# One 1 MB transfer per chunk of the two expert tables, in place of two of 512 KB

## The chip, the cores and the metric

The kernel runs on one core of a Trainium2 chip. The metric is the device time of one execution in microseconds (us). Before the change the median of three runs is 2290.37 us (2289.84 to 2294.24).

## What is computed

The reference is one layer of a hybrid encoder block on 256 tokens of width 2048, all in float32. The part that the change touches is the last and largest one, the PEER layer:

```python
q = jnp.einsum('bsd,de->bse', x, wq).reshape(B, S, PEER_HEADS, 2, PEER_HALF)
...
vals, pos = lax.top_k(cand, PEER_TOPK)
ids = jnp.take_along_axis(cidx, pos, axis=-1)
gates = jax.nn.softmax(vals, axis=-1)
...
ug = jnp.take(u_tab, ib, axis=0)
vg = jnp.take(v_tab, ib, axis=0)
h = jnp.einsum('td,tkd->tk', xb, ug)
a = (jax.nn.gelu(h.astype(jnp.float32), approximate=False) * gb).astype(xb.dtype)
return jnp.einsum('tk,tkd->td', a, vg)
```

There are 128 x 128 = 16384 experts, each a row of 2048 numbers in the table u and one in the table v, 128 MB a table. Each token picks 128 of them (8 heads, 16 each). The kernel gathers nothing. It computes every token's product with every expert of u, multiplies by a gate that is zero for experts that were not picked, and multiplies the result with all of v. So both tables are streamed once through the matrix engine. The layer before it (input projection, pooling, attention, gates, output projection) streams its weights in the same way.

## The kernel before

**Units and chunks.** Every weight matrix is cut into units of 128 x 1024 floats (512 KB). There are 770 of them, and they pass through one pipeline in one order. Two units are a chunk: 128 experts of u or of v. The tables are 128 chunks each, so 256 units each. Table u has the units from 258, table v (called vtab, in the arrays peer_v) those from 514.

**The pipeline of a unit n.** Float32 products are made of float32r parts, so each unit is split in two.

- SyncE (SP) loads it into RAW slot n % 4 (`load`, L320 to L324). It waits first for `lo_ready`, which says that DVE has finished with the unit that was in this slot, n - 4.
- ScalarE (ACT) copies it to HI slot n % 4 (`conv`, L492 to L498), after its landing and after the matmuls of unit n - 4. I write HI(n).
- VectorE (DVE) subtracts and gives the rest, LO slot n % 2 (`conv`, L832 to L839), after HI(n) and after the matmuls of unit n - 2. I write LO(n). It raises `lo_ready`.
- TensorE (PE) multiplies HI (L1493, in vtab L1511) and then LO (L1499, in vtab L1518), and raises `unit_done`.

**What else stands between these steps.** Each engine takes its instructions in program order. ACT converts three units ahead of PE (`ACT_LEAD`), DVE one ahead (`DVE_LEAD`). In between they take the sums of finished chunks out of PSUM. Chunk c of a phase has the units 2c and 2c + 1, counted from the start of its phase:

- Stage A (first 64 chunks of u). ACT: HI(2c + 4), then the copy of chunk c's sums from PSUM (L740), then HI(2c + 5), then gelu (L748). DVE: LO(2c + 1), a piece of the top-k work, LO(2c + 2), another piece, then the join of chunk c (L947, it adds the second half of the sums and waits for ACT's copy), then LO(2c + 3).
- Stage B (last 64 chunks of u). ACT: HI(2c + 4), then the copy of chunk c's sums to HID (L783), then gelu (L786) after DVE's join. DVE: LO(2c + 2), the join of chunk c (L947), `spread` (L1351), one-hots (L1327 and L1331), the product with the gelu (L1344), then LO(2c + 3). PE also makes gate products (L1788).
- vtab. ACT: `a_hi` (L796), HI, HI. DVE: LO, `a_lo` (L1411), LO. The sums stay in PSUM until the end, so no chunk's sums are taken out.

GpSimd loads small things and clears memory; it is not on the path of the units.

Of the kernel before, what the change touches and what calls it, by code (L numbers as in the profile page):

```python
# [31 lines left out]
NK = 128  # L32
# [10 lines left out]
BASE = {}  # L43
# [64 lines left out]
def hybrid_block_kernel(nc, a, out):  # L108
    with ExitStack() as ctx:
        def sem(name):  # L110
            return ctx.enter_context(nc.semaphore(name))
# [8 lines left out]
        def nxt(name, shape, dt=F32):  # L120
            w = word[0]
            word[0] += -(-int(np.prod(shape[1:])) * mybir.dt.size(dt) // 32) * 8
            return at(name, shape, w, dt)
# [3 lines left out]
        RAW = nxt("raw", [P, 4, UNIT])  # L127
# [91 lines left out]
        raw_in = [sem(f"raw_in{s}") for s in range(4)]  # L219
        hi_ready = sem("hi_ready")  # L220
        lo_ready = sem("lo_ready")
# [77 lines left out]
        def val(i, per, k):  # L299
            return k if i is None else i * per + k  # L300
# [9 lines left out]
        @block.sync  # L310
        def _(sp):
            for tt in range(NT):
                sp.dma_start(X0[:, tt, :], a["x"][tt * P:(tt + 1) * P, :]).then_inc(x_in[tt], 16)
            def norm_cols(q):
                for n in range(2):
                    sp.dma_start(LNG[:, n, q * 512:(q + 1) * 512],
                                 bass.AP(tensor=a["ln_in"].tensor, offset=n * D + q * 512, ap=[[0, P], [1, 512]])
                                 ).then_inc(ln_cols_in[q], 16)

            def load(i, per, u, src):  # L320

                if u >= 4 or i is not None:
                    sp.wait_ge(lo_ready, val(i, per, u - 3))
                sp.dma_start(RAW[:, u % 4, :], src).then_inc(raw_in[u % 4], 16)  # L324

            def load_v(u):
                g, ch = u // 2, u % 2
                if u >= 4:
                    sp.wait_ge(lo_ready, u - 3)
                sp.dma_start(RAW[:, u % 4, :].rearrange("p (b c) -> p b c", b=4),  # L330
                             a["w_in"][24 + 4 * ch:28 + 4 * ch, :, g * 256:(g + 1) * 256]
                             .rearrange("b p c -> p b c")).then_inc(raw_in[u % 4], 16)

            norm_cols(0)
            load_v(0)
            load_v(1)
            norm_cols(1)
            load_v(2)
            load_v(3)
            norm_cols(2)  # L340
            norm_cols(3)
            for u in range(4, 16):
                load_v(u)

            blocks = {"qk": 8, "pool": 0, "gate": 32}

            def src(name, i, c, half):
                cols = slice(half * UNIT, (half + 1) * UNIT)
                k = val(i, 2, c)
                if name in blocks:  # L350
                    return a["w_in"][blocks[name] + k, :, cols]
                if name == "vtab":
                    return a["peer_v"][:, k, cols]
                return a[name][k, :, cols]

            for name, n in PHASES[1:]:
                b = BASE[name]
                if name == "grp":
                    continue
                if name == "gate":  # L360
                    with sp.Fori(0, 14) as i:
                        for j in range(4):
                            load(i, 4, b + j, src(name, i, j // 2, j % 2))
                    for t, (c, half) in enumerate(LAST_GATES):
                        load(None, 4, b + 56 + t, src("grp", None, 0, half) if c is None else src(name, None, c, half))
                    continue
                first = 0
                if name == "branch":
                    for j in range(4):
                        load(None, 4, b + j, src(name, None, j % 2, j // 2))  # L370
                    first = 1
                if name in ("wout", "pleg"):
                    for half in range(2):
                        with sp.Fori(0, KD // 4) as i:
                            for j in range(4):
                                k = i * 4 + j
                                load(i, 4, b + KD * half + j, a[name][k, :, half * UNIT:(half + 1) * UNIT])
                    continue
                with sp.Fori(first, n // 2) as i:
                    for j in range(4):  # L380
                        load(i, 4, b + j, src(name, i, j // 2, j % 2))
            sp.wait_ge(spill_out, 32)
            for tt in range(NT):
                for half in range(2):
                    cols = slice(half * (D // 2), (half + 1) * (D // 2))
                    sp.wait_ge(out_ready, 2 * tt + half + 1)
                    sp.dma_start(out[0, tt * P:(tt + 1) * P, cols], RES2[:, tt, cols]).then_inc(out_done, 16)
            sp.wait_ge(out_done, 16 * 2 * NT)
# [102 lines left out]
        def _(act):  # L491
            def conv(i, per, u):  # L492

                act.wait_ge(raw_in[u % 4], 16 * val(i, per // 4, u // 4 + 1))
                if u >= 4 or i is not None:

                    act.wait_ge(unit_done, val(i, per, u - 3))
                nc.scalar.activation(HI[:, u % 4, :], RAW[:, u % 4, :], ACT.Copy).then_inc(hi_ready, 1)  # L498

            def run(name, iters, per, slots, pre=None, start=0, stop=None):  # L500

                b = BASE[name]

                def body(i):
                    for j in range(per):
                        if pre and j % 2 == 0:
                            pre(i, j // 2)
                        conv(i, per, b + j + ACT_LEAD)
                        if j in slots:
                            slots[j](i)  # L510

                if iters == 1:
                    body(None)
                    return
                with act.Fori(start, iters if stop is None else stop) as i:
                    body(i)
# [12 lines left out]
            nc.scalar.activation(BR[0:HEADS, :], PS[0:HEADS, 0, :], ACT.Copy).then_inc(rel_sb, 1)  # L529
            std_of(1)  # L530
            conv(None, 4, 0)
            xt_hi(0, (0,))
            for u in range(1, 4):
                conv(None, 4, u)
# [1348 lines left out]
```

## Time and profile before

| | |
|---|---|
| median of 3 runs | 2290.37 us |
| profiled execution, its own time | 2288.23 us |
| its span (first to last instruction) | 2286.6 us |
| PE busy | 2241.0 us (98%) |
| DVE busy | 1530.6 us (67%) |
| ACT busy | 1067.3 us (47%) |
| DMA | 425.40 MB, mean 186 GB/s |
| chain that ended last | PE 92%, DVE 4%, issue 2%, DMA 1% |

Busy time is the time in which an engine had an instruction running. The chain that ended last follows the work back from the last instruction, at each step to what released it. PEclk in a row is the TensorE clock that was granted, as a share of full speed. Line numbers are those of the kernel before. L498, L838 and L947 are lines of helpers that serve many places, so a row is told apart by what it writes and reads.

### The profile page before, as it was taken

To read this page: it belongs to the slowest core of one execution; us is meant where nothing else is said; L and a number is where in the kernel's file an instruction comes from. 1 tells how busy PE (TensorE), PEld (TensorE's weight loads), DVE (VectorE), ACT (ScalarE), POOL (GpSimd) and SP (SyncE) were. 2 spreads that over 40 slices of the span, in tenths; PEclk is the share of its full clock that TensorE was granted. 3 is DMA by queue.
4 is the path that set the end of the run, shared out by engine and by line. 5 is a ranking of instruction groups with operands and counts; after the bars stand their busy time and mean duration, and the time that the engine had idled before them with its cause. 6 is when DMAs were issued, how large, how long until landed. Compare 5 with 4: busy or idle time off the path is not lost.

```text
span 2286.6 us, 39059 instructions
## 1 busy us (share of the span) xinstructions
PE 2241.0 (98%) x12096; PEld 1932.4 (85%) x12096; DVE 1530.6 (67%) x2818; ACT 1067.3 (47%) x1483; POOL 45.9 (2%) x93
## 2 busy tenths in 40 slices
PE   7999999999999999999999999999999999999996
PEld 5888888998888888888888888888888888888885
DVE  6457666765744599998888888887555555555556
ACT  3444555654444444445554444444444444444442
POOL 1000000000000000011000000000000000000000
PEclk9999999999999999999999999999999999999998
DMA  7555555557465556565555555555666666666663
GB/s 265 187 189 173 178 183 173 185 196 249 146 192 178 174 185 199 186 210 187 189 160 164 162 163 158 160 163 175 193 192 197 202 205 205 202 202 202 202 192 120
DMA packets 122729, 425.40 MB, mean 186 GB/s; under 512 B 13448, under 2 KB 21656, under 8 KB 121792
## 3 DMA queue, kind: packets, MB, share of 16 engines
q1 hardware_dynamic: 119040, 410.04, 56.1%
q0 software_dynamic: 3648, 14.82, 2.0%
q8 instruction: 25, 0.41, 0.1%
q14 instruction: 16, 0.13, 0.0%
HBM read 420.60 MB, written 6.31 MB: 187 GB/s over the span
## 4 chain that ended last, share of the span: by engine, by line
PE 92%; DVE 4%; issue 2%; DMA 1%; ACT 0%; DVEq 0%; SPq 0%; ACTq 0%
PE ps L1493 29%; PE ps L1511 25%; PE ps L1499 15%; PE ps L1518 13%; PE ps L1788 3%; PE ps L1557 1%; PE ps L1476 1%; PE ps L1481 1%; PE ps L1477 1%; DVE w_lo L838 1%; PE ps L1563 1%; DMA raw<-in_w_in 1%; DVE bn L850 0%; DMA x<-in_x 0%; PE ps L1538 0%
## 5 line engine op out<-in xcount | busy, mean ns | idle before, releaser
L838 DVE TENSOR_TENSOR w_lo<-raw,w_hi 128x1024 fp32r<-128x1024 f32 x770 | 940.3, 1222 | 455.7 <-PE ps L1518 388.9
L498 ACT ACTIVATE w_hi<-raw 128x1024 fp32r<-128x1024 f32 x770 | 815.7, 1061 | 907.0 <-DMA raw<-in_peer_v 372.4
L1493 PE MATMUL ps<-x_t_hi_lo,w_hi 128*128 128x512 f32 x3200 | 815.9, 397 | 1.2 <-DVE experts L947 1.2
L1493 PEld LDWEIGHTS ps<-x_t_hi_lo,w_hi 128*128 128x128 f32 x3200 | 574.0, 189 | 107.1 <-issue 2.7
L1511 PE MATMUL ps<-w_hi,x_t_hi_lo 128*128 128x512 f32 x2560 | 633.2, 389 | 1.3 <-DVE x_t_hi_lo L1411 1.2
L1511 PEld LDWEIGHTS ps<-w_hi,x_t_hi_lo 128*128 128x128 f32 x2560 | 479.8, 188 | 101.0 <-issue 1.8
L1499 PEld LDWEIGHTS ps<-x_t_hi_lo,w_lo 128*128 128x128 f32 x3200 | 435.1, 190 | 38.7 <-DVE w_lo L838 6.8
L1499 PE MATMUL ps<-x_t_hi_lo,w_lo 128*128 128x256 f32 x3200 | 446.8, 282 | 2.3 <-DVE w_lo L838 2.1
L1518 PE MATMUL ps<-w_lo,x_t_hi_lo 128*128 128x512 f32 x1280 | 342.3, 389 | 1.0 <-DVE w_lo L838 1.0
L1518 PEld LDWEIGHTS ps<-w_lo,x_t_hi_lo 128*128 128x128 f32 x1280 | 240.2, 188 | 51.3 <-DVE w_lo L838 1.4
L1788 PE MATMUL ps<-onehots 128*128 128x128 f32 x512 | 77.0, 274 | 0.0
L1331 DVE TENSOR_SCALAR onehots<-iota,i_t,gate_t 128x128 f32<-128x128 bf16 x256 | 76.7, 344 | 0.0
L1788 PEld LDWEIGHTS ps<-onehots 128*128 128x128 f32 x512 | 68.0, 192 | 0.0
L1327 DVE TENSOR_TENSOR onehots<-i_t,iota 128x256 f32<-128x256 bf16 x128 | 53.9, 421 | 19.0 <-DVE experts L1351 14.9
L1411 DVE TENSOR_TENSOR x_t_hi_lo<-experts,x_t_hi_lo 128x256 fp32r<-128x256 f32 x128 | 53.5, 418 | 1.0 <-ACT x_t_hi_lo L796 0.9
L796 ACT ACTIVATE x_t_hi_lo<-experts 128x256 fp32r (+1 forms) x128 | 51.1, 400 | 1.0 <-PE ps L1499 1.0
L947 DVE TENSOR_TENSOR hidden<-ps,hidden 128x256 f32<-128x256 f32 x64 | 27.1, 424 | 28.9 <-ACT hidden L783 28.9
L786 ACT ACTIVATE hidden<-hidden 128x256 f32<-128x256 f32 x64 | 26.8, 419 | 36.5 <-DVE hidden L947 36.5
L783 ACT ACTIVATE hidden<-ps 128x256 f32<-128x256 f32 x64 | 24.6, 384 | 41.0 <-PE ps L1499 40.9
L1351 DVE TENSOR_TENSOR experts<-ps,experts 128x512 f32 (+1 forms) x64 | 43.5, 680 | 0.0
L947 DVE TENSOR_TENSOR gates_t<-ps,gates_t 128x256 f32 (+1 forms) x32 | 13.5, 422 | 41.4 <-ACT gates_t L552 39.8
L947 DVE TENSOR_TENSOR experts<-ps,experts 128x256 f32 x64 | 27.2, 424 | 16.6 <-ACT experts L740 10.6
(214 smaller groups left out, 1126.8 us busy)
## 6 DMA issues: line engine op xcount, KB each, us to landing
raw<-in_u SPq DMA_DIRECT2D x256, 512.0 KB, 4.3
raw<-in_peer_v SPq DMA_DIRECT2D x256, 512.0 KB, 4.7
raw<-in_w_in SPq DMA_DIRECT2D x128, 512.0 KB, 4.3
raw<-in_branch SPq DMA_DIRECT2D x32, 512.0 KB, 4.8
raw<-in_wout SPq DMA_DIRECT2D x32, 512.0 KB, 4.8
raw<-in_pleg SPq DMA_DIRECT2D x32, 512.0 KB, 4.2
raw<-in_wq SPq DMA_DIRECT2D x32, 512.0 KB, 4.2
x<-in_x SPq DMA_DIRECT2D x2, 1024.0 KB, 6.6
```

Source lines behind the costliest of these rows:

```text
L498: nc.scalar.activation(HI[:, u % 4, :], RAW[:, u % 4, :], ACT.Copy).then_inc(hi_ready, 1)
L796: nc.scalar.activation(XH[:, c % 4, :], BUF[:, bass.ds(val(i, 4, c), 1), :].rearrange("p a t -> p (a t)"), ACT.Copy).then_inc(ah_ready, 1)
L838: v.tensor_tensor(LO[:, u % 2, :], RAW[:, u % 4, :], HI[:, u % 4, :].bitcast(F32), ALU.subtract) \
L947: v.tensor_tensor(dst, PS[:, bank, S:2 * S], dst, ALU.add).then_inc(joined, 1)
L1327: ch.tag(v.tensor_tensor(OH[:, n % 2, :, 0, :], both.unsqueeze(2).to_broadcast([P, 2, P]), IOTA[:, :].unsqueeze(1).to_broadcast([P, 2, P]) ...
L1331: ins = v.tensor_scalar(OH[:, n % 2, r, 1, :], IOTA[:, :], I2T[:, bass.ds(t, 1)], GATET[:, bass.ds(t, 1)], ALU.is_equal, ALU.mult)
L1411: v.tensor_tensor(XL[:, c % 4, :], BUF[:, bass.ds(val(i, 4, c), 1), :].rearrange("p a t -> p (a t)"), XH[:, c % 4, :].bitcast(F32), ALU.su ...
L1493: mm(PS[:, bank, :], w(HI, u % 4)[:, k, :], XHL[:, 8 * half + k, :, :].rearrange("p a t -> p (a t)"), start=(half == 0 and k == 0), stop=F ...
L1499: r = mm(PS[:, bank, 0:S], w(LO, u % 2)[:, k, :], XH[:, 8 * half + k, :], start=False, stop=(half == 1 and k == 7))
L1511: mm(nbank(tt, 2 * half + q), stn[:, tt * P:(tt + 1) * P], wh[:, q * 512:(q + 1) * 512], start=(first and s == 0), stop=False, skip_group_ ...
L1518: r = mm(nbank(tt, 2 * half + q), ah[:, tt * P:(tt + 1) * P], wl[:, q * 512:(q + 1) * 512], start=False, stop=last, skip_group_check=True)
L1788: r = mm(PS[:, 4 + g % 2, o:o + P], OH[:, n % 2, t, 0, :], OH[:, n % 2, t, 1, :], start=True, stop=True)
```

## The change

For u and vtab, SP issues one transfer of 128 x 2048 floats (1 MB) per chunk, into the RAW slots of both its units, and ACT waits for the semaphore of the first slot for both. The wait ahead of the transfer is for both slots: `lo_ready` must say that LO of unit u - 3 is done, the unit that was in the second slot. The first chunk of u is still loaded in two parts. All other phases are as before.

```diff
+            def load_chunk(name, i, b, c):
+
+                u = b + 2 * c
+                sp.wait_ge(lo_ready, val(i, 4, u - 2))
+                whole = a["u"][val(i, 2, c)] if name == "u" else a["peer_v"][:, val(i, 2, c), :]
+                sp.dma_start(RAW[:, u % 4:u % 4 + 2, :], whole.rearrange("p (h c) -> p h c", h=2)
+                             ).then_inc(raw_in[u % 4], 16)
+
...
+                if name in ("u", "vtab"):
+                    if name == "u":
+                        load(None, 4, b, src(name, None, 0, 0))
+                        load(None, 4, b + 1, src(name, None, 0, 1))
+                        load_chunk(name, None, b, 1)
+                    with sp.Fori(1 if name == "u" else 0, NK // 2) as i:
+                        load_chunk(name, i, b, 0)
+                        load_chunk(name, i, b, 1)
+                    continue
...
-                act.wait_ge(raw_in[u % 4], 16 * val(i, per // 4, u // 4 + 1))
+                slot = 2 * (u % 4 // 2) if u >= BASE["u"] else u % 4
+                act.wait_ge(raw_in[slot], 16 * val(i, per // 4, u // 4 + 1))
```

SP's instructions in the loop over u before, two chunks an iteration (ISA is the wait for `lo_ready`):

```order
L324 ISA [waits lo_ready]
L324 DMA raw<-in_u 128x1024
L323 REGISTER_ALU
L324 ISA [waits lo_ready]
L324 DMA raw<-in_u 128x1024
L323 REGISTER_ALU
L324 ISA [waits lo_ready]
L324 DMA raw<-in_u 128x1024
L323 REGISTER_ALU
L324 ISA [waits lo_ready]
L324 DMA raw<-in_u 128x1024
```

and in the changed kernel, also two chunks:

```order
L361 ISA [waits lo_ready]
L361 DMA raw<-in_u 128x2048
L359 REGISTER_ALU
L361 ISA [waits lo_ready]
L361 DMA raw<-in_u 128x2048
```

Two of four waits are gone, those that let the first half of a chunk go ahead of the second.

ACT at the start of stage A before. The rows are HI of an even unit (2c + 4), the copy of chunk c's sums, HI of the odd unit (2c + 5), gelu, and the same again:

```order
L498 ACTIVATE w_hi<-raw 128x1024 [waits unit_done,raw_in2]
L740 ACTIVATE experts<-ps 128x256 [waits unit_done]
L498 ACTIVATE w_hi<-raw 128x1024 [waits unit_done,raw_in3]
L748 ACTIVATE experts<-experts 128x256 [waits joined]
L498 ACTIVATE w_hi<-raw 128x1024 [waits unit_done,raw_in0]
L740 ACTIVATE experts<-ps 128x256 [waits unit_done]
```

and the same place in the changed kernel, where L516 is the old L498 and L758 the old L740:

```order
L516 ACTIVATE w_hi<-raw 128x1024 [waits unit_done,raw_in2]
L758 ACTIVATE experts<-ps 128x256 [waits unit_done]
L516 ACTIVATE w_hi<-raw 128x1024 [waits unit_done,raw_in2]
L766 ACTIVATE experts<-experts 128x256 [waits joined]
L516 ACTIVATE w_hi<-raw 128x1024 [waits unit_done,raw_in0]
L758 ACTIVATE experts<-ps 128x256 [waits unit_done]
```

No instruction of ACT has moved; the odd unit now waits for the semaphore of the even one's slot.

DVE in the stage A loop of the changed kernel, from the join of one chunk (L965, before L947) to LO of its odd unit (L856, before L838). DVE's order is the same in both kernels:

```order
L965 ISA [waits act_evac]
L965 TENSOR_TENSOR experts<-ps,experts 128x256
L852 REGISTER_ALU
L856 TENSOR_TENSOR w_lo<-raw,w_hi 128x1024 [waits unit_done,hi_ready]
L1231 MAX tk_v<-tk_s 128x8 x2
```

The join waits for ACT's copy, and the next LO stands right behind the join.

## Rows read from the trace of the kernel before

**Rows 1.** The page: span, and shares of the chain that ended last.

```profile
span 2286.6 us, 39059 instructions
...
PE 92%; DVE 4%; issue 2%; DMA 1%; ACT 0%; DVEq 0%; SPq 0%; ACTq 0%
```

**Rows 2.** Windows: us; busy of PE, PEld, DVE, ACT, POOL; PEclk, DMA share, GB/s.

```profile
1120.00:1530.00 410.00, 408.85 (x2504) 364.72 (x2503) 347.19 (x728) 189.21 (x260) 2.59 (x5) 1.00 0.51 163
1530.00:2230.00 700.00, 698.80 (x3154) 581.13 (x3153) 375.29 (x442) 311.68 (x391) 8.60 (x16) 1.00 0.64 197
```

**Rows 3.** Timeline, stage A: start, us, engine, line, [idle before <-releaser].

```profile
1000.44 1.21 DVE L838 TENSOR_TENSOR w_lo<-raw,w_hi 128x1024 fp32r<-128x1024 f32 x1
1000.95 2.00 PE L1493 MATMUL ps<-x_t_hi_lo,w_hi 128*128 128x512 f32 x8
...
1001.82 11.07 SPq L324 DMA_DIRECT2D raw<-in_u  x5
...
1002.92 1.06 ACT L498 ACTIVATE w_hi<-raw 128x1024 fp32r<-128x1024 f32 x1 [1.41 <-DMA raw<-in_u]
...
1004.05 0.39 ACT L740 ACTIVATE experts<-ps 128x256 f32 x1
...
1005.29 0.43 DVE L947 TENSOR_TENSOR experts<-ps,experts 128x256 f32 x1
...
1005.63 1.22 DVE L838 TENSOR_TENSOR w_lo<-raw,w_hi 128x1024 fp32r<-128x1024 f32 x1
...
1006.54 2.00 PE L1493 MATMUL ps<-x_t_hi_lo,w_hi 128*128 128x512 f32 x8
```

**Rows 4.** Timeline, stage B.

```profile
1506.21 0.38 ACT L783 ACTIVATE hidden<-ps 128x256 f32<-128x256 f32 x1 [0.38 <-PE ps L1499]
...
1506.30 2.09 PE L1493 MATMUL ps<-x_t_hi_lo,w_hi 128*128 128x512 f32 x8
1506.63 0.42 DVE L947 TENSOR_TENSOR hidden<-ps,hidden 128x256 f32<-128x256 f32 x1 [0.26 <-ACT hidden L783]
...
1509.26 1.23 DVE L838 TENSOR_TENSOR w_lo<-raw,w_hi 128x1024 fp32r<-128x1024 f32 x1 [0.19 <-DVE experts L1344]
...
1512.79 2.09 PE L1493 MATMUL ps<-x_t_hi_lo,w_hi 128*128 128x512 f32 x8
1513.12 0.42 DVE L947 TENSOR_TENSOR hidden<-ps,hidden 128x256 f32<-128x256 f32 x1 [0.66 <-ACT hidden L783]
...
1516.15 1.23 DVE L838 TENSOR_TENSOR w_lo<-raw,w_hi 128x1024 fp32r<-128x1024 f32 x1 [0.21 <-DVE experts L1344]
```

**Rows 5.** Landing of the two 1 MB transfers of x at the start.

```profile
DMA to landing us min/median/max: 5.0/6.6/8.2
```

**Rows 6.** Landing of 123 transfers of u in stage B, 512 KB each.

```profile
DMA to landing us min/median/max: 3.4/3.9/5.2
```

**Rows 7.** DMA issues of the page: KB each, median us to landing.

```profile
raw<-in_u SPq DMA_DIRECT2D x256, 512.0 KB, 4.3
raw<-in_peer_v SPq DMA_DIRECT2D x256, 512.0 KB, 4.7
```

**Rows 8.** Timeline, vtab.

```profile
2000.54 1.98 PE L1511 MATMUL ps<-w_hi,x_t_hi_lo 128*128 128x512 f32 x8
2000.81 1.22 DVE L838 TENSOR_TENSOR w_lo<-raw,w_hi 128x1024 fp32r<-128x1024 f32 x1 [1.16 <-PE ps L1518]
...
2002.42 0.40 ACT L796 ACTIVATE x_t_hi_lo<-experts 128x256 fp32r x1
...
2003.26 1.98 PE L1511 MATMUL ps<-w_hi,x_t_hi_lo 128*128 128x512 f32 x8
...
2004.60 0.42 DVE L1411 TENSOR_TENSOR x_t_hi_lo<-experts,x_t_hi_lo 128x256 fp32r<-128x256 f32 x1
```

**Rows 9.** Windows at the end, after the last matmul; columns as in rows 2.

```profile
2265.00:2269.00 4.00, 0.00 (x0) 0.00 (x0) 3.96 (x8) 0.00 (x0) 0.00 (x0) 1.00 0.00 0
2269.00:2286.00 17.00, 0.00 (x0) 0.00 (x0) 14.03 (x19) 0.20 (x1) 0.00 (x0) 0.50 0.31 123
```

## The prediction

> **What bounds the kernel now.** I read the page first. The reader sees there that PE holds 92% of the chain that ended last, of a span of 2286.6 us [rows 1]. The windows by stage say the same of the parts that change: PE is busy 408.85 of 410 us in stage B of u and 698.80 of 700 in vtab, at a clock of 1.00 [rows 2]. So no stall is there to be removed. A change of the loads can gain next to nothing, and the question is whether PE stays fed. For that I read the timeline of a few units in each stage, for the order in which SP, ACT and DVE release each other [rows 3, 4, 8], and then the landing times [rows 5 to 7].
>
> PE spends 1006.54 - 1000.95 = 5.59 us on a chunk in stage A [rows 3], 1512.79 - 1506.30 = 6.49 in stage B [rows 4], and 2 x (2003.26 - 2000.54) = 5.44 in vtab [rows 8].
>
> **What the change removes.** Half of SP's transfers of the tables, 256. SP has nothing else to do in these stages and is not on the chain [rows 1]. Gain: nothing. The bytes are the same.
>
> **What it moves.** The transfer of chunk c + 2 (units 2c + 4 and 2c + 5) now leaves after LO(2c + 1). Before, its first half left after LO(2c), a unit earlier, and was half as long. Three things on the way decide what that costs.
>
> 1. ACT takes HI(2c + 4) right ahead of the copy of chunk c's sums: 1002.92 and 1004.05 in stage A [rows 3]. It takes instructions in order, so the copy waits for the landing.
> 2. DVE's join of chunk c waits for that copy.
> 3. DVE's LO(2c + 3) is behind the join: 1005.29 and 1005.63 [rows 3].
>
> LO(2c + 3) is what the next transfer waits for. So a loop closes over one chunk: LO(2c + 1), transfer, HI, copy, join, LO(2c + 3), next transfer. Before, the same path ran from LO(2c) to LO(2c + 3), three units of PE's time for it, and with the shorter transfer. Now it has two.
>
> **The length X of a 1 MB transfer.** No row shows one of a table. Three nearest rows: the first transfer of x has this size and shape and took 5.0 us from issue to landing, with little beside it [rows 5]. The second, 8.2, lay behind the first. 512 KB of u take 3.4 to 5.2 us in stage B, median 3.9 [rows 6]. To add the second half: the DMA engines move 163 GB/s at a busy share of 0.51 [rows 2], so 320 at full, and 0.52 MB take 1.64 us. That gives 3.4 + 1.64 = 5.0 at best and 3.9 + 1.64 = 5.5 at the median; the median holds transfers that met another one, and in the loop there is only one in flight. I take 5.2, and 4.8 to 5.7 as bounds.
>
> The Trainium skill (DMA: Bandwidth & Descriptors, Measured) has 6.15 us for 1 MB, and a fit of 2.0 us + bytes / 436e3, which is 4.4 us; its rule is to batch transfers to 1 MiB or more. With 6.15 the sum below would be an estimated 120 us longer, with 4.4 an estimated 100 shorter. The row of x lies between them.
>
> **Stage A, one loop.** LO's end to the issue: 1001.82 - 1001.65 = 0.17. X = 5.2. ACT's start after the landing: 0.10 (an allowance; DVE's start behind ACT's copy in rows 4 is of this kind). HI 1.06. Copy 0.07 behind it, 0.39. DVE starts 0.04 later (1506.59 to 1506.63 in [rows 4]). From the join's start to LO's end 1005.29 to 1006.85: 1.56 [rows 3]. Sum 0.17 + 5.2 + 0.10 + 1.06 + 0.07 + 0.39 + 0.04 + 1.56 = 8.6 us, against 5.59 of PE's work. Each chunk costs 3.0 us more. DVE's other work between the joins (the top-k pieces and LO(2c + 2)) is ahead of the join, and fits into the wait for the transfer: from LO's end at 1001.65 to the join at 1005.29 it takes at most 3.6 us [rows 3], and the copy now comes 5.2 + 1.8 = 7.0 us after LO. So that work adds nothing.
>
> **Stage B, one loop.** The same up to the copy (0.38, L783). Behind it DVE has more ahead of LO(2c + 3): join, spread, one-hots, the product. From the join's start to LO's end 1506.63 to 1510.49 = 3.86 and 1513.12 to 1517.38 = 4.26, mean 4.06 [rows 4]. Sum 0.17 + 5.2 + 0.10 + 1.06 + 0.07 + 0.38 + 0.04 + 4.06 = 11.1 us, against 6.49. Each chunk costs 4.6 us more.
>
> **vtab.** No sums are taken out there, so nothing of ACT or DVE for chunk c stands behind a landing of chunk c + 2. Two chunks have 4 slots, so the loop is over two chunks, 10.88 us: issue 0.17, X, 0.10, HI 1.06, a_hi 0.40, a_lo 0.42, two LO at 1.22 [rows 8], together X + 4.6. It is hidden if X is under 6.3. The halves take 4.7 there [rows 7], at 2.72 us from each other, so always two in flight; 4.7 + 1.64 = 6.3 is the upper bound, 5.2 the value as above. I cost vtab at nothing. PE's work hides it, and every 0.1 us over 6.3 would cost 64 x 0.1 = 6 us.
>
> **Sum.** The loop applies from the first full 1 MB transfer on: 65 loops of kind A (one of them with wq's last copy), 64 of kind B. 65 x 3.0 + 64 x 4.6 = 195 + 294 = 489. At the edges of stage B DVE has less between join and LO, some 8 us less in all by my reading of the program. 480 us on top of the profiled 2288 are 2768; the median of the runs shown lies 2 us above that execution. I predict **2770 us**.
>
> **The rivals.**
>
> *The transfers are hidden (not slower).* If 1 MB landed early enough for the loop to fit under PE's work, the time would stay at 2290. This decides below X = 5.2 - 3.0 = 2.2 us in stage A and 5.2 - 4.6 = 0.6 in stage B. Even 512 KB need 3.4 [rows 6]. For it speaks only that I could have misread what ACT or DVE stands behind. Same: 3 in 100. Gain: 2 in 100; with 1.15 us of PE idle in stage B and 1.2 in vtab [rows 2] it could be some 3 us at most, unless the larger transfers let the engines run undisturbed, of which no row tells.
>
> *PE's clock falls.* PE would now be idle 11.1 - 6.49 = 4.6 us in each chunk of stage B and 3.0 in A. At the end of the kernel the clock is still 1.00 in a window of 4 us without a matmul, and 0.50, that is 1.2 GHz, in the next [rows 9]. So gaps of B are about as long as what brought it down, those of A shorter. A dip costs nothing by itself: PE's late matmuls eat its own gap. Only if the clock stays at half through the stage does PE become the bound, at 2 x 6.49 = 13.0 a chunk in B: (13.0 - 11.1) x 64 = 120 us more, 2890. With A too, 2 x 5.59 = 11.2, another (11.2 - 8.6) x 65 = 170, 3060. The Trainium skill (TensorE: Matmul & The Clock Gate, HAM oscillation) tells of a kernel in which each wait for a transfer brought the clock down again; by that rule the time is that of this rival. Against it: PE works 60% of the time, and then runs back to back. 9 in 100.
>
> *vtab's loop binds too.* With X = 6.8 there, 64 x 0.5 = 32 us more: 2800. For it speaks the 4.7 us of [rows 7], against it that this came with two in flight. 10 in 100.
>
> *The forecast*, 76 in 100. Its own range: X from 4.8 to 5.7 is 129 x 0.4 = 52 us down and 129 x 0.5 = 65 up, and 0.2 to 0.3 us a loop for waits that I have not seen another 25 down or 35 up: 2690 to 2870. That also holds the vtab rival, so I take it as the range. Below and above it remain the hidden case (5) and the clock (9), and a little of the tails.
>
> **Chances.** A measurement of this kernel tells changes over about 0.2% from none. Faster 0.02, same 0.03, slower 0.95.
>
> **What the profile after would show.** Landing of 1 MB at about 5.2 us after issue in stages A and B. In both, PE's idle time ahead of the LO matmuls (L1499's successor) of odd units, about 3.0 and 4.6 us a chunk, released by DVE's LO; DVE's join waiting for ACT's copy; ACT's HI waiting for the DMA. Stage A some 555 us long, stage B some 710, vtab as before with PE without gaps. If ACT's copy or DVE's join does not wait, step 1 or 2 is wrong. If it does and the sum is off, X is. A granted clock under 1.00 in stage B would speak for the clock.

## The result and the profile after

The changed kernel takes 2709.6 us (median of 4 runs, 2708.45 to 2710.57) against 2290.1 us of the kernel before on the same chip: a ratio of 1.183, 95% interval 1.1816 to 1.1844. It is 420 us slower.

Of the page after, the rows that answer to [rows 1]: the span, the granted TensorE clock in 40 equal slices, the shares of the chain that ended last, PE's LO matmuls (L1517, the old L1499), and the two costliest idle places of DVE's join (L965, the old L947). The number behind the last bar is the engine's idle time ahead of these instructions, with what ended it.

```profile
span 2708.8 us, 38028 instructions
...
PEclk9999999999998898999888888888899999999998
...
PE 54%; DMA 22%; DVE 12%; issue 7%; ACT 2%; DVEq 1%; SPq 1%; ACTq 1%
...
L1517 PE MATMUL ps<-x_t_hi_lo,w_lo 128*128 128x256 f32 x3200 | 490.9, 299 | 253.1 <-DVE w_lo L856 253.1
...
L965 DVE TENSOR_TENSOR hidden<-ps,hidden 128x256 f32<-128x256 f32 x64 | 27.2, 425 | 270.2 <-ACT hidden L801 270.2
...
L965 DVE TENSOR_TENSOR experts<-ps,experts 128x256 f32 x64 | 27.2, 425 | 186.2 <-ACT experts L758 186.2
```

The same row of PE before:

```profile
L1499 PE MATMUL ps<-x_t_hi_lo,w_lo 128*128 128x256 f32 x3200 | 446.8, 282 | 2.3 <-DVE w_lo L838 2.1
```

PE held 92% of the chain before and holds 54% now; transfers, DVE and ACT have 36%. DVE's joins wait 456 us for ACT's copies. PE waits 253 us for LO, where it waited 2. That is less than the 420 us that were lost, because PE also has the same 12096 matmuls running for 2396 us, where it took 2241: some run at the lower clock. What that is worth is the fifth experiment.

Windows of stage A, stage B and vtab (columns as in [rows 2]):

```profile
795.00:1303.00 508.00, 400.43 (x1970) 325.75 (x1969) 310.21 (x990) 161.83 (x246) 15.37 (x30) 0.92 0.37 131
1325.00:1970.00 645.00, 498.86 (x2507) 425.36 (x2506) 345.44 (x695) 173.85 (x252) 1.92 (x4) 0.86 0.28 101
```

```profile
2000.00:2600.00 600.00, 600.00 (x2649) 496.99 (x2648) 307.31 (x332) 254.82 (x330) 8.60 (x16) 1.00 0.58 200
```

The loss is in the two stages of u and, for some 10 us, in the passage from u to vtab (sixth experiment). Within vtab PE is busy in every microsecond. The issues of the 1 MB transfers give the length of a loop. First stage A, then stage B, then vtab: how many, the first and the last start, and the time to landing.

```profile
L361 SPq DMA_DIRECT2D raw<-in_u x62: 332/333/343, 795.2 to 1300.7; - x62
...
DMA to landing us min/median/max: 4.6/4.8/6.7
```

```profile
L361 SPq DMA_DIRECT2D raw<-in_u x62: 332/333/333, 1325.4 to 1960.8; - x62
...
DMA to landing us min/median/max: 4.6/4.8/4.9
```

```profile
L361 SPq DMA_DIRECT2D raw<-in_peer_v x123: 332/333/333, 1970.0 to 2644.6; - x123
...
DMA to landing us min/median/max: 4.9/5.1/6.6
```

From the first issue to the last there are 61 loops in each stage of u. Stage A: 505.5 us, or 8.29 a loop. Stage B: 635.4 us, or 10.42. Against PE's 5.59 and 6.49 of [rows 3, 4] that is 65 x 2.70 + 64 x 3.93 = 427 us, near the measured 420.

One loop of stage B in the timeline, from the release of a transfer to the next (it answers to [rows 4]):

```profile
1604.64 1.22 PE L1517 MATMUL ps<-x_t_hi_lo,w_lo 128*128 128x256 f32 x8 [1.86 <-DVE w_lo L856]
1604.76 11.00 SPq L361 DMA_DIRECT2D raw<-in_u  x2
...
1606.23 3.52 PE L1511 MATMUL ps<-x_t_hi_lo,w_hi 128*128 128x512 f32 x8
...
1609.63 1.06 ACT L516 ACTIVATE w_hi<-raw 128x1024 fp32r<-128x1024 f32 x1 [7.01 <-DMA raw<-in_u]
...
1610.59 0.36 ACT L801 ACTIVATE hidden<-ps 128x256 f32<-128x256 f32 x1
...
1610.99 0.42 DVE L965 TENSOR_TENSOR hidden<-ps,hidden 128x256 f32<-128x256 f32 x1 [4.41 <-ACT hidden L801]
...
1614.02 1.23 DVE L856 TENSOR_TENSOR w_lo<-raw,w_hi 128x1024 fp32r<-128x1024 f32 x1 [0.21 <-DVE experts L1362]
...
1615.30 1.41 PE L1517 MATMUL ps<-x_t_hi_lo,w_lo 128*128 128x256 f32 x8 [2.32 <-DVE w_lo L856]
```

Read it down the left column, in order of time. The transfer is issued at 1604.76. ACT has waited 7.01 us when it lands, and starts HI at 1609.63. The copy follows at 1610.59, the join at 1610.99 after 4.41 us of waiting, and LO ends at 1614.02 + 1.23 = 1615.25. PE has waited 2.32 us for it. The row of SP holds two issues, each of 0.33 us: the second comes at 1604.76 + 11.00 - 0.33 = 1615.43, and the loop is closed.

### The profile page after: what moved, and what is told of

Its sections match the earlier page's. It is cut to its first block, busy times and chain, and to the rows that moved or that the text cites. A ratio compares the mean times of both kernels' runs of the same rounds, so it can differ in the third digit from the quotient of the medians.

```text
span 2708.8 us, 38028 instructions
## 1 busy us (share of the span) xinstructions
PE 2396.1 (88%) x12096; PEld 2023.6 (75%) x12096; DVE 1532.2 (57%) x2818; ACT 1032.9 (38%) x1483; POOL 45.7 (2%) x93
## 4 chain that ended last, share of the span: by engine, by line
PE 54%; DMA 22%; DVE 12%; issue 7%; ACT 2%; DVEq 1%; SPq 1%; ACTq 1%
PE ps L1529 21%; DMA raw<-in_u 20%; PE ps L1536 11%; PE ps L1511 10%; DVE w_lo L856 6%; PE ps L1517 6%; DVE experts L1369 2%; PE ps L1494 1%; PE ps L1499 1%; PE ps L1495 1%; DVE onehots L1349 1%; ACT experts L758 1%; DMA raw<-in_w_in 1%; PE ps L1575 1%; DVE experts L1362 1%
## 5 line engine op out<-in xcount | busy, mean ns | idle before, releaser
L516 ACT ACTIVATE w_hi<-raw 128x1024 fp32r<-128x1024 f32 x770 | 812.0, 1056 | 1433.0 <-DMA raw<-in_u 778.1
L856 DVE TENSOR_TENSOR w_lo<-raw,w_hi 128x1024 fp32r<-128x1024 f32 x770 | 940.1, 1222 | 264.2 <-PE ps L1536 197.9
L1511 PE MATMUL ps<-x_t_hi_lo,w_hi 128*128 128x512 f32 x3200 | 892.6, 425 | 5.7 <-DVE experts L965 5.7
L1511 PEld LDWEIGHTS ps<-x_t_hi_lo,w_hi 128*128 128x128 f32 x3200 | 629.5, 207 | 128.4 <-DVE experts L965 5.9
L1517 PE MATMUL ps<-x_t_hi_lo,w_lo 128*128 128x256 f32 x3200 | 490.9, 299 | 253.1 <-DVE w_lo L856 253.1
L1517 PEld LDWEIGHTS ps<-x_t_hi_lo,w_lo 128*128 128x128 f32 x3200 | 455.0, 202 | 335.2 <-DVE w_lo L856 311.8
L1529 PE MATMUL ps<-w_hi,x_t_hi_lo 128*128 128x512 f32 x2560 | 634.5, 390 | 3.2 <-DVE x_t_hi_lo L1429 3.1
L965 DVE TENSOR_TENSOR hidden<-ps,hidden 128x256 f32<-128x256 f32 x64 | 27.2, 425 | 270.2 <-ACT hidden L801 270.2
L965 DVE TENSOR_TENSOR experts<-ps,experts 128x256 f32 x64 | 27.2, 425 | 186.2 <-ACT experts L758 186.2
L1806 PE MATMUL ps<-onehots 128*128 128x128 f32 x512 | 95.8, 322 | 8.8 <-DVE onehots L1349 8.8
L1806 PEld LDWEIGHTS ps<-onehots 128*128 128x128 f32 x512 | 85.1, 235 | 9.4 <-DVE onehots L1349 9.4
L1575 PE MATMUL ps<-w_hi,x_t_hi_lo 128*128 128x512 f32 x128 | 34.4, 413 | 3.6 <-issue 2.5
L965 DVE TENSOR_TENSOR gates_t<-ps,gates_t 128x256 f32 (+1 forms) x32 | 13.5, 423 | 41.6 <-ACT gates_t L570 39.9
```

Source lines behind the costliest of these rows:

```text
L856: v.tensor_tensor(LO[:, u % 2, :], RAW[:, u % 4, :], HI[:, u % 4, :].bitcast(F32), ALU.subtract) \
L965: v.tensor_tensor(dst, PS[:, bank, S:2 * S], dst, ALU.add).then_inc(joined, 1)
L1511: mm(PS[:, bank, :], w(HI, u % 4)[:, k, :], XHL[:, 8 * half + k, :, :].rearrange("p a t -> p (a t)"), start=(half == 0 and k == 0), stop=F ...
L1517: r = mm(PS[:, bank, 0:S], w(LO, u % 2)[:, k, :], XH[:, 8 * half + k, :], start=False, stop=(half == 1 and k == 7))
L1529: mm(nbank(tt, 2 * half + q), stn[:, tt * P:(tt + 1) * P], wh[:, q * 512:(q + 1) * 512], start=(first and s == 0), stop=False, skip_group_ ...
L1575: mm(o[tt], x[:, 2 * g + k, tt * P:(tt + 1) * P], w(HI, u % 4, k), start=(g == 0 and k == 0 and x is XH), stop=False, skip_group_check=True)
```

## The experiments

The theory: a loop over one chunk, closed because ACT takes HI(2c + 4) ahead of the copy of chunk c. The rivals: 1 MB is late or costly by itself, wherever it stands; the later issue of the first half is all; PE's clock is a part of it. The kernels and their results, each against the kernel before on the same chip:

| kernel | us, median | ratio, 95% interval |
|---|---|---|
| changed, ACT's order turned in u | 2298.34 | 1.0034 (1.002 to 1.0048) |
| 1 MB in vtab alone | 2300.16 | 1.0042 (1.0028 to 1.0056) |
| two halves, both late | 2593.0 | 1.1319 (1.13 to 1.1338) |
| early halves, wait for both | 2575.73 | 1.1247 (1.1228 to 1.1266) |
| changed, filler matmuls | 2710.46 | 1.1828 (1.1808 to 1.1848) |
| before, ACT's order turned | 2289.61 | 0.9997 (0.9987 to 1.0006) |
| changed, turned in stage A alone | 2542.25 | 1.1098 (1.1079 to 1.1116) |
| changed, turned everywhere | 2294.11 | 1.0016 (1.0007 to 1.0025) |
| 1 MB in vtab alone, passage turned | 2291.15 | 1.0005 (0.9996 to 1.0014) |

### 1. Take the copy out of the loop

In this and the other diffs pieces are left out, and "..." marks the place. The first piece is stage A, the second stage B; the gelu of stage B moves with the copy. The first of the two chunks in the passage to vtab is turned in the same way, the second is not.

```diff
+                        if name == "u" and j % 2:
+                            sums_a(j // 2)(i)
+                            conv(i, per, b + j + ACT_LEAD)
+                            if j == 7:
+                                gelu_a(3)(i)
+                            continue
                         conv(i, per, b + j + ACT_LEAD)
                         if j in slots:
...
-                    conv(i, 4, BASE["u"] + 2 * TOPK_CHUNKS + j + ACT_LEAD)
                     if j % 2:
                         gelu_chunk(i, j // 2)
+                    conv(i, 4, BASE["u"] + 2 * TOPK_CHUNKS + j + ACT_LEAD)
```

> The changed kernel, with ACT's order turned round at one place: in both stages of u, ACT takes chunk c's sums out of PSUM (in stage B the gelu too) ahead of HI(2c + 4) and not behind it. The 1 MB transfers and their waits stay. Theory (the loop over one chunk through ACT's copy and DVE's join): the copy no longer waits for a landing, so LO(2c + 3) doesn't either. The loop is then over two chunks, some 10.1 us in A and 11.5 in B against 11.3 and 13.0 of PE's work: 2290 to 2310 us, PE without gaps. Rival (DVE and PE starve because 1 MB is simply late, whatever ACT's order): HI(2c + 4) comes no earlier than now, so 2700 us or more. Rival (the clock's dips are part of the loss): they would go with the gaps, so this run can't tell it from the theory; the filler run does.

2298.34 us. 411 of the 420 us are gone, with every transfer of 1 MB and every wait of SP still there. In its trace PE is busy 330.00 of 330 us in a stretch of stage B:

```profile
1200.00:1530.00 330.00, 330.00 (x2035) 294.87 (x2034) 280.19 (x560) 143.00 (x203) 0.00 (x0) 1.00 0.45 161
```

The rival that 1 MB is late whatever ACT's order falls. 8 us are left; the last two runs look for them.

### 2. The same turn in the kernel before

> The kernel before with the same turn of ACT's order as in the first run, transfers of 512 KB as they were. It says what the turn does by itself. Theory: PE has no gaps to give back, and the copy was not late: 2288 to 2292 us. Rival (the turn is a gain of its own that hides a loss of the 1 MB transfers): faster than 2285.

2289.61 us, ratio 0.9997 (0.9987 to 1.0006). The turn has no gain of its own that could hide a loss.

### 3. One stage at a time

The first edit in stage A alone.

> The changed kernel with ACT's order turned round in stage A alone; stage B keeps copy and gelu behind HI. Theory: stage A falls to PE's 5.6 us a chunk, stage B stays at 10.4: 2290 + 64 x 3.9 = 2540 us. Rival (one stage's loss is passed on from the other, or is not made by the loop): any other split, such as 2290 or 2710.

2542.25 us, 2 us above the 2540 of the theory. Windows of stage A and of stage B of this kernel:

```profile
800.00:1120.00 320.00, 317.37 (x1808) 276.75 (x1807) 286.83 (x910) 151.88 (x226) 14.99 (x29) 1.00 0.53 192
1200.00:1750.00 550.00, 424.56 (x2106) 361.15 (x2104) 288.47 (x578) 145.76 (x212) 0.00 (x0) 0.85 0.28 100
```

PE is busy for all but 2.6 of 320 us in the stage whose copy is ahead of HI, and has the gaps (and the low clock) in the other. The passage to vtab is not turned here. So stage B with the passage makes 252 us of the loss, and stage A the rest, 167.

### 4. What the loop is made of

Two halves of 512 KB with a semaphore each, both issued after the wait of the changed kernel:

```diff
-                sp.dma_start(RAW[:, u % 4:u % 4 + 2, :], whole.rearrange("p (h c) -> p h c", h=2)
-                             ).then_inc(raw_in[u % 4], 16)
+                for h in range(2):
+                    sp.dma_start(RAW[:, u % 4 + h, :], whole[:, h * UNIT:(h + 1) * UNIT]
+                                 ).then_inc(raw_in[u % 4 + h], 16)
...
-                slot = 2 * (u % 4 // 2) if u >= BASE["u"] else u % 4
+                slot = u % 4
```

> The changed kernel's wait, but two transfers of 512 KB right behind each other after it, each with its own semaphore, and ACT waits for each alone. Theory: the loop over one chunk stays, with the landing of the first half in it in place of X = 4.8: 3.9 to 4.2 us with the second half beside it. 129 x 0.6 to 0.9 us less: 2595 to 2630. Rival (the length of one transfer is all that costs, and the later issue is covered): 2290 to 2320. Rival (the later issue is all): 2700 to 2710.

2593.0 us, 117 less than the changed kernel or 0.90 us a loop: 4.8 - 0.9 = 3.9 us in the loop. Taken transfer by transfer, its trace agrees: in stage B the first halves land in 3.9 us at the median and the second halves, issued right behind them, in 4.6. The time is 2 us below the range that I expected.

The kernel before with its early issues, where ACT's HI of an even unit waits for both halves:

```diff
                 act.wait_ge(raw_in[u % 4], 16 * val(i, per // 4, u // 4 + 1))
+                if u >= BASE["u"] + 2 and u % 2 == 0:
+                    act.wait_ge(raw_in[u % 4 + 1], 16 * val(i, per // 4, u // 4 + 1))
```

> The kernel before, with its two transfers of 512 KB at their early times, but ACT's HI of a chunk's first unit waits for both halves. Theory: LO(2c + 1) lets the second half go, and HI(2c + 4) waits for it, so the loop over one chunk closes here too, with 512 KB in it, alone in flight: 3.6 us in place of 4.8. 129 x 1.2 = 155 us less than the changed kernel: 2555 us. Rival (the later issue of the first half is what costs): 2290. Rival (only the larger transfer costs): 2290 too.

2575.73 us. That is 134 us under the changed kernel, 1.04 a loop, so some 3.7 to 3.8 us of landing and not the 3.6 that I put in: 21 us over my number. One loop of stage B in its trace, and the transfer that it turns on, issued at 1499.45:

```profile
L324 SPq DMA_DIRECT2D raw<-in_u x1: 332/332/332, 1499.4 to 1499.4; - x1
...
DMA to landing us min/median/max: 3.7/3.7/3.7
```

```profile
1503.37 1.06 ACT L500 ACTIVATE w_hi<-raw 128x1024 fp32r<-128x1024 f32 x1 [6.30 <-DMA raw<-in_u]
...
1504.34 0.37 ACT L785 ACTIVATE hidden<-ps 128x256 f32<-128x256 f32 x1
...
1504.74 0.42 DVE L949 TENSOR_TENSOR hidden<-ps,hidden 128x256 f32<-128x256 f32 x1 [3.48 <-ACT hidden L785]
...
1507.36 1.23 DVE L840 TENSOR_TENSOR w_lo<-raw,w_hi 128x1024 fp32r<-128x1024 f32 x1 [0.19 <-DVE experts L1346]
...
1508.64 2.07 PE L1501 MATMUL ps<-x_t_hi_lo,w_lo 128*128 128x256 f32 x8 [2.56 <-DVE w_lo L840]
```

The half in the loop lands in 3.7 us at the median in both stages. I had expected it alone in flight, and it is not: the next chunk's first half leaves some 2 us behind it.

This run says most. Each half is issued on the same condition as in the kernel before, no transfer is larger, and still 285 us are lost. It is enough that HI(2c + 4) waits for something that LO(2c + 1) releases. So of the 420 us, the loop with a half transfer in it makes some 285 to 303, and the longer transfer adds the rest.

### 5. The clock

Eight more matmuls (2.0 us in the trace) between HI and LO of each odd unit of u, into a bank that nobody reads:

```diff
+                    if half == 1 and u >= BASE["u"]:
+                        for k in range(8):
+                            mm(PS[:, 1, :], w(HI, u % 4)[:, k, :],
+                               XHL[:, 8 * half + k, :, :].rearrange("p a t -> p (a t)"),
+                               start=(k == 0), stop=(k == 7))
```

> The changed kernel, and PE makes eight more matmuls of 128x512 (1.9 us, into a PSUM bank that nobody reads) between HI and LO of each odd unit of u, in the gap where it waits for LO. They add work and take none away. PE's work is then 7.5 us a chunk in A and 8.4 in B, under the loops of 8.3 and 10.4, and its idle stretches are shorter, so the clock should stay at 1.00 more. Theory (a dip falls into PE's own gap and costs nothing): time unchanged, 2700 to 2720 us, at a higher mean clock. Rival (the dips cost a part of the 420 us): faster by that part; at half clock a third of stage B's PE work would come back, 50 us or more: under 2660.

2710.46 us. Windows of stages A and B of this kernel:

```profile
795.00:1303.00 508.00, 476.75 (x2476) 391.32 (x2475) 311.02 (x993) 161.84 (x246) 15.41 (x30) 1.00 0.37 132
1325.00:1970.00 645.00, 555.49 (x2994) 469.87 (x2994) 343.33 (x692) 172.35 (x250) 1.92 (x4) 0.96 0.28 101
```

The granted clock rose from 0.92 to 1.00 in A and from 0.86 to 0.96 in B, and the time did not move. The dips to 1.2 GHz are real: in the timeline above eight matmuls that take 2.09 us at full clock take 3.52. But PE then only waits less: its idle time in stage B's window goes from 645.00 - 498.86 = 146 us to 645.00 - 555.49 = 90, with the loop as long as it was. In these two stages, where PE isn't the bound, the dips cost nothing that the time shows.

### 6. vtab, and the passage to it

1 MB transfers in vtab alone.

> 1 MB transfers in vtab alone, table u loaded in halves as before. Theory: vtab's loop is over two chunks and hidden with X = 5.2 us: 2288 to 2293 us. Rival (1 MB transfers cost something wherever they stand, by the slots that they hold or by contention): 1/2 of the loss is here, 2290 + 210 = 2500.

2300.16 us, 10 us more than before: neither number. Along vtab nothing is lost (first row, the passage; second, 600 us of vtab):

```profile
1560.00:1586.00 26.00, 19.48 (x86) 16.09 (x85) 13.12 (x22) 7.16 (x12) 0.00 (x0) 0.80 0.33 117
1600.00:2200.00 600.00, 600.00 (x2648) 496.81 (x2647) 306.85 (x332) 254.84 (x330) 8.60 (x16) 1.00 0.58 200
```

The passage is where ACT still takes the last two chunks of u out of PSUM behind HI of vtab's first and third unit. Its timeline has the same loop, twice:

```profile
1563.48 1.06 ACT L516 ACTIVATE w_hi<-raw 128x1024 fp32r<-128x1024 f32 x1 [6.26 <-DMA raw<-in_peer_v]
...
1566.89 1.84 PE L1806 MATMUL ps<-onehots 128*128 128x128 f32 x8 [2.43 <-DVE onehots L1349]
...
1574.64 1.06 ACT L516 ACTIVATE w_hi<-raw 128x1024 fp32r<-128x1024 f32 x1 [7.92 <-DMA raw<-in_peer_v]
...
1576.79 3.75 PE L1529 MATMUL ps<-w_hi,x_t_hi_lo 128*128 128x512 f32 x8 [3.96 <-DVE x_t_hi_lo L1429]
```

PE idles 2.43 and 3.96 us, 6.4 of the 10. Behind that the clock is down: eight matmuls take 3.75 us, 1.98 in [rows 8]. Here PE is the bound right away, so I put the rest to the low clock; no run takes the two apart.

The last two kernels turn ACT's order in the passage, for both of its chunks:

```diff
             for j in range(4):
-                conv(None, 4, vb - 4 + j + ACT_LEAD)
                 if j == 3:
                     act.wait_ge(g_used, 64)
                     act.wait_ge(unit_done, vb - 1)
                     a_hi(None, 0)
                 if j % 2:
                     gelu_chunk(B_ITERS - 1, j // 2)
+                conv(None, 4, vb - 4 + j + ACT_LEAD)
```

> 1 MB transfers in vtab alone, as in the run of that kind, with ACT's order turned round in the passage from u to vtab only (both its chunks). Theory (its 10 us were lost in the passage, not along vtab): 2288 to 2293 us. Rival (they are spread over vtab): 2300.

2291.15 us, ratio 1.0005 (0.9996 to 1.0014): the 10 us were in the passage.

> The first run's kernel (1 MB transfers in u and vtab, ACT's order turned round in both stages of u) and the turn made at the last place too, the passage from u to vtab: ACT takes a_hi of chunk 0 and the last chunk's sums ahead of HI of vtab's third unit. Theory (the 8 us that the first run lost are the same loop, closed twice in this passage, with PE idle 5.0 us and then at half clock for 6.8): 2288 to 2293 us, no gap over 1.3 us in the passage. Rival (1 MB transfers cost 8 us along vtab or u): 2298.

2294.11 us, ratio 1.0016 (1.0007 to 1.0025). The passage is repaired, but 4 us remain, and the time is 1 us above the range that I expected. One part shows in stage A of this kernel, at the two places where GpSimd's store of x is in flight beside a 1 MB load of u. These two loads land in 6.4 and 6.7 us. The second:

```profile
980.08 1.92 POOL L488 MEMSET experts<- 128x512 f32 x4 [4.83 <-DMA residual_dram<-x]
...
982.60 2.01 ACT L516 ACTIVATE w_hi<-raw 128x1024 fp32r<-128x1024 f32 x2 [5.23 <-DMA raw<-in_u]
...
983.70 1.66 PE L1521 MATMUL ps<-x_t_hi_lo,w_hi 128*128 128x512 f32 x6 [1.29 <-ACT w_hi L516]
```

PE waited for HI at both, 2.2 us in all, and does not in the kernel before, which makes the same stores. The profiled execution, at 2291.88 us, is the fastest of the eleven, so the other 2 us may not be in it at all; what makes them isn't settled. No version is faster than the kernel before: PE, busy for 98% of its span, has next to nothing to give.

## Why the prediction was right, and its sizes

**The steps.** The three steps of the loop hold as they were put: the copy waits for HI and the landing, the join for the copy, LO for the join. Taking the copy out from behind HI takes 411 us back. PE's gaps, DVE's waits for ACT's copy and ACT's for the transfer are where the prediction had them. The loops are 8.29 and 10.42 us for the predicted 8.6 and 11.1, and the result stands near the lower end of the range. PE's idle time is smaller than the 3.0 and 4.6 us a chunk that I named as a sign: 107.6 of 508 us and 146.1 of 645, or 1.8 and 2.4 a loop. The sign left out what I say of the clock myself: late matmuls fill a part of PE's own gap.

**The length X of the transfer.** The term that was mis-sized most is this one. I took 5.2 us, and the runs show 4.8 at the median. 129 x 0.4 = 52 us of the 60 between 2770 and 2710 are this. Even my lower end by the rows, 3.4 + 1.64 = 5.0, was too long. The 1.64 came from a rate of 320 GB/s that I got by dividing by the busy share. A half in the loop took 3.7 us in the early-halves kernel, so the second half adds some 1.1 us. Why that rate came out too low was not tested. The Trainium skill (DMA: Bandwidth & Descriptors) has a fit (Anatomy of one DMA — SWDGE (gpsimd) path) that gives an estimated 4.4 us for 1 MB, and a table (Measured) with 6.15, both for transfers that GpSimd issues. SP issues these; their 4.8 us are nearer to the fit.

**The copy.** I had it start 0.07 us behind HI. When ACT has waited for HI, the copy is ready and starts before HI has ended: 1610.59 against 1609.63 + 1.06 = 1610.69. Some 0.17 us a loop, 22 us less. Stage A gives some of it back in three places: the join starts 0.15 us behind the copy and not 0.04, in every fourth loop one more instruction of DVE stands between join and LO (0.3 to 0.6 us), and two of the transfers met GpSimd's stores and took 6.3 and 6.7 us.

**vtab.** Right, and its rival with X = 6.8 wrong: 5.1 us of landing at the median against a limit of 6.3, and PE without gaps. I had treated the passage between u and vtab as two more loops. It is that, and a clock that is low just when PE becomes the bound.

**The rivals.** The transfers were not hidden. The clock fell, to a mean of 0.86 over stage B, but did not stay at half, and the filler run shows that it cost nothing there. It also fell in stage A, to 0.92, where I had called the gaps shorter than the 4 us of [rows 9]: a wait of 2.32 us is followed by eight matmuls in 3.52 us, where [rows 3] has 2.00.

```profile
1004.02 1.21 PE L1517 MATMUL ps<-x_t_hi_lo,w_lo 128*128 128x256 f32 x8 [2.32 <-DVE w_lo L856]
...
1005.06 3.52 PE L1511 MATMUL ps<-x_t_hi_lo,w_hi 128*128 128x512 f32 x8
```

The Trainium skill (TensorE: Matmul & The Clock Gate, HAM oscillation) tells that waits for transfers bring the clock down again. This trace agrees for a part of the waits; what it costs depends here on whether PE is the bound.

## What to carry to other kernels

Before you merge transfers, find what releases the merged one and what stands behind its landing on each in-order engine. If the consumer's evacuation of an older tile is queued behind the conversion of the new one, the landing time enters a loop with the release. By the order of the instructions one more pair of slots would let the transfer go a chunk earlier and make this a loop over two chunks; no run here has it. Count that loop in units of work (here it shrank from three units to two) and put the evacuation ahead of the wait: in this kernel that is a change of order in ACT's program, worth 411 us.

## What the runs showed of the hardware beyond that

A 1 MB load with 8 KB rows, alone in flight, took 4.6 to 4.9 us in all 62 cases of stage B, against 3.7 us for half of it in the loop of the early-halves kernel. In vtab the same 200 GB/s kept the DMA engines busy at a share of 0.58 (the kernel with 1 MB in vtab alone, above) in place of 0.65 in the same stretch of the kernel before:

```profile
1600.00:2200.00 600.00, 600.00 (x2648) 496.81 (x2647) 307.26 (x331) 267.29 (x332) 8.60 (x16) 1.00 0.65 200
```

So the larger transfers keep the engines that carry them less busy, and this kernel had no use for it. Whether that is the longer rows (8 KB, not 4 KB) or the smaller number of transfers, no run here tells.
